# A table of 256 x 16,384 expert weights: written by GpSimd's accumulating indirect transfers instead of by one-hot products on TensorE

## What is computed

```python
qry = (af @ w_q).reshape(n, PEER_HEADS, 2, PEER_KEY_DIM)            # 8 heads
s = jnp.einsum('nhpd,hpkd->nhpk', qry, sub_keys)                    # two times 128 keys
s_top, i_top = lax.top_k(s, PEER_TOPK)                              # 16 of 128, twice
cand = s_top[:, :, 0, :, None] + s_top[:, :, 1, None, :]
sc, ci = lax.top_k(cand.reshape(n, PEER_HEADS, 256), PEER_TOPK)     # 16 of 256 pairs
experts = e_a * PEER_N_KEYS + e_b                                   # 8 x 16 = 128 per token
gw = jax.nn.softmax(sc, axis=-1)
act = jax.nn.gelu(jnp.einsum('td,tkd->tk', xb, u_tab[experts]))
out = jnp.einsum('tk,tkd->td', gw * act, v_tab[experts])
```

## Time and profile before

| | before |
|---|---|
| median of 3 runs | 1804.25 us (1803.99 to 1805.73) |
| span of the profiled execution | 1795.7 us |
| PE busy | 1744.2 us, 97% |
| DVE, ACT, POOL busy | 1251.2, 942.1, 492.9 us |
| TensorE's granted clock, mean | 0.994 |
| DMA bytes | 347.63 MB, mean 194 GB/s |

### The profile page before, as it was taken

How to read it: one execution, slowest core, us unless ns; L and a number is a source line. 1 busy time by engine, 2 the same in 40 slices (tenths; PEclk the granted TensorE clock), 3 DMA queues, 4 the chain that set the end, 5 groups by cost and what they waited for, 6 DMA issues and landing times.

```text
span 1795.7 us, 33010 instructions
## 1 busy us (share of the span) xinstructions
PE 1744.2 (97%) x11190; PEld 1547.2 (86%) x11190; DVE 1251.2 (70%) x2359; ACT 942.1 (52%) x1389; POOL 492.9 (27%) x225
## 2 busy tenths in 40 slices
PE   9999989999999999999999999999999999999997
PEld 6799878897878999999999988888888787669996
DVE  4567587876424499067777578888888896667777
ACT  5466577544555544567777643333333575334444
POOL 4246744401568588800000000000000100013332
PEclk9999999999999999999999999999999999999999
DMA  6654443577344478755565687677767783355553
GB/s 216 200 188 141 166 152 118 190 248 266 121 164 150 135 222 228 228 179 172 174 173 173 195 263 239 235 235 236 237 239 236 272 276 122 113 176 187 183 183 113
DMA packets 122839, 347.63 MB, mean 194 GB/s; under 512 B 13904, under 2 KB 46800, under 8 KB 122512
## 3 DMA queue, kind: packets, MB, share of 16 engines
q1 hardware_dynamic: 121248, 339.52, 58.1%
q0 software_dynamic: 1520, 7.21, 1.1%
HBM read 328.84 MB, written 17.83 MB: 193 GB/s over the span
## 4 chain that ended last, share of the span: by engine, by line
PE 84%; DVE 6%; ACT 4%; issue 2%; POOL 2%; DMA 1%; POOLq 0%; DVEq 0%; ACTq 0%
PE banks L934 83%; POOL weight_rest L851 2%; ACT arena L1676 2%; DMA weight_ring<-in_stream 1%; ACT weight_high L1676 1%; PE banks L945 1%; DVE weight_rest L2307 1%; ACT span_exponentials L1676 0%; DVE arena L3110 0%; DVE arena L2991 0%; DVE arena L2348 0%; ACT scratch L1676 0%; ACT L1676 0%; DVE arena L2347 0%; DVE arena L2345 0%
## 5 line engine op out<-in xcount | busy, mean ns | idle before, releaser
L1676 ACT ACTIVATE weight_high<-weight_ring 128x1024 fp32r<-128x1024 f32 x448 | 473.0, 1057 | 453.4 <-PE banks L934 350.4
L851 POOL TENSOR_TENSOR weight_rest<-weight_ring,weight_high 128x1024 fp32r<-128x1024 f32 x165 | 414.4, 2521 | 264.5 <-ACT weight_high L1676 155.0
L2307 DVE TENSOR_TENSOR weight_rest<-weight_ring,weight_high 128x1024 fp32r<-128x1024 f32 x283 | 346.1, 1224 | 156.3 <-ACT weight_high L1676 153.4
L934 PE MATMUL banks<-a_high,weight_high 128*128 128x256 f32 x1216 | 304.0, 288 | 0.2 <-ACT weight_high L1676 0.2
L934 PE MATMUL banks<-a_rest,weight_high 128*128 128x256 f32 x1216 | 297.8, 283 | 0.0
L934 PEld LDWEIGHTS banks<-a_high,weight_high 128*128 128x128 f32 x1216 | 232.6, 191 | 1.5 <-issue 1.1
L934 PEld LDWEIGHTS banks<-a_rest,weight_high 128*128 128x128 f32 x1216 | 232.9, 192 | 0.3 <-issue 0.2
L934 PE MATMUL banks<-weight_high,gated_high 128*128 128x512 f32 x512 | 201.4, 393 | 0.0
L934 PE MATMUL banks<-weight_high,gated_rest 128*128 128x512 f32 x512 | 200.2, 391 | 0.0
L934 PE MATMUL banks<-a_high,weight_rest 128*128 128x256 f32 x1216 | 170.9, 283 | 2.4 <-POOL weight_rest L851 2.4
L934 PE MATMUL banks<-x_high,weight_high 128*128 128x256 f32 x672 | 167.5, 287 | 4.7 <-DVE x_rest L3079 3.7
(11 more groups left out here) (360 smaller groups left out, 3101.5 us busy)
## 6 DMA issues: line engine op xcount, KB each, us to landing
weight_ring<-in_stream SPq DMA_DIRECT2D x512, 512.0 KB, 3.5
arena<-in_stream SPq DMA_DIRECT2D x66, 512.0 KB, 3.3
unit_spill<-small SPq DMA_DIRECT2D x128, 128.0 KB, 3.6
scratch<-unit_spill SPq DMA_DIRECT2D x128, 128.0 KB, 3.2
residual<-in_x SPq DMA_DIRECT2D x2, 512.0 KB, 4.1
arena<-in_mem POOLq DMA_DIRECT2D x2, 512.0 KB, 5.3
arena<-in_ctx POOLq DMA_DIRECT2D x2, 512.0 KB, 4.8
arena<-in_keys POOLq DMA_DIRECT2D x1, 1024.0 KB, 5.2
```

The costliest lines, as they stand in the source:

```text
L851: nc.gpsimd.tensor_tensor(w_lo[:, e % 2, :], raw(e)[0], w_hi[:, e % 2, :], ALU.subtract).then_inc(S["rest_ready"], 1)
L934: return nc.tensor.matmul(out, lhsT, rhs, start=start, stop=stop, skip_group_check=True)
L1676: return nc.scalar.activation(out, in_, f, **kw)
L2307: tt(w_lo[:, e % 2, :], raw(e)[0], w_hi[:, e % 2, :], ALU.subtract).then_inc(S[ready], 1)
```

## The change

G is built in DRAM. SP first fills `gate_matrix` (16.8 MB) with zeros, in 32 transfers of 512 KB from a block of 64 zeros per partition, one with every third tile of the early stream. DVE makes for each token and choice a number `expert * 256 + token`. POOL makes rests for 36 unit tiles only; then it issues 256 indirect transfers, one for each half of the tokens and each of the 128 choices. Each adds 128 weights, one from each partition, to 128 cells of `gate_matrix`. The 16 choices of a head name different experts; between the heads of one half it waits until the earlier transfers of that half have landed, so that sums are not lost. SP waits for all of them at the first value tile and then loads one row of G (128 KB) beside every value tile. `u2`, the transposes `eTr`, the one-hot matrices and the moves to `WT` are gone; DVE makes the rests of the last 92 unit tiles. Some semaphores are merged.

```diff
-U_EARLY, U_EXP, U_GATED = 52, 48, 64
+U_EARLY = 36
+N_ZERO = 32
@@ SP
+            def load_gates(a):
+                if a >= 4:
+                    sp.wait_ge(g_in[a % 4], 16 * (a // 4))
+                sp.dma_start(WT[:, a, :], gate_matrix[a]).then_inc(g_in[a % 4], 16)
+                if g == 32:
+                    sp.wait_ge(S["warm_zeros"], 2)
+                if g >= 32 and g % 3 == 0 and (g - 32) // 3 < N_ZERO:
+                    sp.dma_start(to_zero[(g - 32) // 3], zeros).then_inc(zeroed, 16)
                 if sec == "values":
                     if i < 6:
                         store_units(P - 6 + i)
+                    if i == 0:
+                        for t in range(TT):
+                            sp.wait_ge(scattered[t], 16 * PSLOT)
+                        for d in range(2):
+                            freed(sp, ("cH", d))
+                        for a in range(3):
+                            load_gates(a)
+                    if i + 3 < P:
+                        load_gates(i + 3)
@@ POOL, behind the rests of the first 36 unit tiles
+            pool.wait_ge(zeroed, 16 * N_ZERO)
+            cells = gate_matrix.rearrange("a b (t o) -> (a b t) o", o=1)
+            for h in range(PH):
+                for t in range(TT):
+                    if h == 0:
+                        pool.wait_ge(S["idx_ready"], t + 1)
+                    else:
+                        pool.wait_ge(scattered[t], 16 * PTOP * h)
+                    for k in range(h * PTOP, (h + 1) * PTOP):
+                        pool.indirect_dma_start(
+                            cells, bass.IndirectOffsetOnAxis(EXPERT_TOKEN[:, t, k:k + 1], 0), EAB[:, t, 2, k:k + 1], None,
+                            compute_op=ALU.add).then_inc(scattered[t], 16)
@@ PE
-            for t in range(TT):
-                pe.wait_ge(S["idx_ready"], t + 1)
-                transposes(("eTr", t), [EAB[:, t, x, :] for x in range(3)])
-            with pe.Fori(0, T // 16) as i:
-                for u in range(4):
-                    units(U_EARLY + u, ("u2", u), i)
...
-                    for v in range(4):
-                        ins = mm(b[:, hsl(v)], COLUMN[:, u % 2, v, :], ROWHOT[:, u % 2, v, :])
             with pe.Fori(0, U_LATE // 4) as i:
                 for j in range(4):
-                    units(U_EARLY + U_GATED + j, ("u3", j), i)
+                    units(U_EARLY + j, ("u3", j), i)
@@ DVE, with the early rests
+            step(V.tensor_reduce(token_numbers[:, 0:1], C("upto"), AX.X, ALU.add))
+            for t in range(TT):
+                ts(token_numbers[:, 1 + t:2 + t], token_numbers[:, 0:1], -1.0, float(P * (t + 1)), ALU.mult, ALU.add)
@@ DVE, end of best_pairs
+                step(stt(OH[:, 0:P], EAB[:, t, 0, :], float(P), EAB[:, t, 1, :], ALU.mult, ALU.add))
+                step(ts(EXPERT_TOKEN[:, t, :], OH[:, 0:P], float(T), token_numbers[:, 1 + t:2 + t], ALU.mult, ALU.add))
@@ DVE, behind the searches
+            split_rest(UD, "lo_ready")
             gates(0)
             gates(1)
-            with dve.Fori(0, T // 16) as i:
-                for u in range(4):
-                    split_rest(UD + u, "lo_ready", i, 4)
...
+            for j in range(1, 4):
+                split_rest(UD + j, "lo_ready")
+            with dve.Fori(0, U_LATE // 4 - 1) as i:
+                for j in range(4, 8):
+                    split_rest(UD + j, "lo_ready", i, 4)
@@ DVE, gate_row
                 dve.wait_ge(h_in[s], i_ * 16 + 16 * (a // 4 + 1))
+                dve.wait_ge(g_in[s], i_ * 16 + 16 * (a // 4 + 1))
```

More of the change, by code:

```diff
@@ L336, in plan_banks @@
     B.loop("u1", U_EARLY // 4, 4, banks=(4, 5, 4, 5))
-    for t in range(TT):
-        B.job("eTr", t, bank=6 + t)
     for d in range(2):
         B.job("cH", d, bank=4 + d)
-    B.loop("u2", U_GATED // 4, 4, banks=(4, 5, 4, 5))
-    B.loop("w", T // 16, 4, banks=(6, 7, 6, 7))
-    B.loop("u3", U_LATE // 4, 4, banks=(4, 5, 6, 7))
+    B.loop("u3", U_LATE // 4, 4, banks=(4, 5, 4, 5))
     B.job("ad1", "rows", 2, bank=4)
@@ L529, in build @@
         h_in = [sem(f"units_loaded{s}") for s in range(4)]
+        g_in = [sem(f"gates_loaded{s}") for s in range(4)]
+        zeroed = sem("gate_matrix_zeroed")
+        scattered = [sem(f"gates_scattered{t}") for t in range(TT)]
         in_x = [sem(f"x_loaded{t}") for t in range(TT)]
@@ L809, in load_units @@
                 sp.dma_start(UNITS_IN[:, a % 4, :], spill[a]).then_inc(h_in[a % 4], 16)
+            def load_gates(a):
+                if a >= 4:
+                    sp.wait_ge(g_in[a % 4], 16 * (a // 4))
+                sp.dma_start(WT[:, a, :], gate_matrix[a]).then_inc(g_in[a % 4], 16)
+            zeros = bass.AP(zero_block[:, :].tensor, zero_block[:, :].offset, [zero_block[:, :].ap[0], [0, 16], [1, 64]])
+            to_zero = gate_matrix.rearrange("a b t -> (a b t)").rearrange("(p n r c) -> n p r c", p=P, n=N_ZERO, c=64)
             for g in range(len(RING_TILES)):
@@ L889, in _ @@
                     split_rest(U0 + j, i, 4)
+            pool.wait_ge(zeroed, 16 * N_ZERO)
[10 more added lines that the diff above has]
+                            compute_op=ALU.add).then_inc(scattered[t], 16)
             for s in range(4):
                 pool.wait_ge(h_out[s], 16 * P // 4)
-            pool.dma_start(FIN1, A["fin1"].partition_broadcast(P)).then_inc(in_gain, 16)
+            pool.dma_start(FIN1, A["fin1"].partition_broadcast(P)).then_inc(in_second, 16)
             arrived(pool, ("x2T", 1, 1))
@@ L898, in _ @@
             pool.dma_start(GSPAN[:, :, :], A["span"]).then_inc(in_second, 16)
-            pool.wait_ge(in_second, 4 * 16)
+            pool.wait_ge(in_second, 5 * 16)
             pool.wait_ge(S["x2_lo_ready"], 4)
@@ L1807, in _ @@
             act.wait_ge(S["dt_abs"], 1)
-            func(NEGA, row("a_log"), ACT.Exp).then_inc(S["neg_a"], 1)
+            func(NEGA, row("a_log"), ACT.Exp).then_inc(S["dt_l"], 1)
             step(func(DTS, DTS, ACT.Exp, scale=-1.0))
@@ L2036, in _ @@
                 split_high(U0 + j + 2)
-            with act.Fori(1, U_EXP // 4) as i:
+            with act.Fori(1, U_EARLY // 4) as i:
                 for j in range(4):
@@ L2044, in _ @@
                 func(EAB[:, t, 2, :], EAB[:, t, 2, :], ACT.Exp).then_inc(S["gate_exp"], 1)
[L2045 to L2051 removed]
             for d in range(2):
                 evacuate(("cH", d), h0[:, d], src=quarters)
[L2055 to L2084 removed]
             with act.Fori(0, U_LATE // 4) as i:
                 for j in range(4):
[L2087 removed]
+                    act.wait_ge(h_out[j], i * 16 + 16 * U_EARLY // 4)
                     unit_out(("u3", j), j, i)
[L2089 removed]
+                    split_high(U0 + U_EARLY + j + 2, i, 4)
             with act.Fori(0, P // 4 - 1) as i:
@@ L2768, in _ @@
             gate_scores(1)
+            split_rest(UD, "lo_ready")
             gates(0)
             gates(1)
-            for t in range(TT):
-                freed(dve, ("eTr", t))
-            ts(slots[:, 3, :], slots[:, 1, :], -1.0, None, ALU.mult).then_inc(S["slots_negated"], 1)
-            with dve.Fori(0, T // 16) as i:
-                for u in range(4):
-                    split_rest(UD + u, "lo_ready", i, 4)
-                    b, n = B.at[("w", (u - 2) % 4)]
-                    dve.wait_ge(bank_full[b], i * 2 + (n if u >= 2 else n - 2))
-                    for v in range(4):
-                        slot = bass.ds(i * 16 + (4 * u + v), 1)
-                        ins = ts(ROWHOT[:, u % 2, v, :], C("iota"), slots[:, 0, slot], slots[:, 2, slot],
-                                 ALU.is_equal, ALU.mult)
-                    ins.then_inc(S["onehot_ready"], 1)
-                    if u:
-                        quad = bc(slots[:, 1, bass.ds(i * 16 + 4 * u, 4)], 2, P)
-                        tt(COLUMN[:, u % 2], bc(C("iota"), 1, 4), quad, ALU.is_equal).then_inc(S["dve_columns"], 1)
-            with dve.Fori(0, U_LATE // 4) as i:
-                for j in range(4):
-                    split_rest(UD + U_GATED + j, "lo_ready", i, 4)
-            for u in range(4):
-                freed(dve, ("w", u), T // 16 - 1)
+            for j in range(1, 4):
[3 more added lines that the diff above has]
+                    split_rest(UD + j, "lo_ready", i, 4)
             def gate_row(a, turn=None):
```

82 lines of the change are left out of this document (21 added, 61 removed).

## The result

The changed kernel takes **2023.55 us** (median of 4 runs, 2022.43 to 2026.78) against 1804.38 us before (4 runs, 1803.99 to 1805.73): 1.1219 times the time, 95% interval 1.1203 to 1.1235. The prediction said 1775.6 us, 1747 to 1895. It missed by 248 us, and the time lies outside its range. The profiled execution has a span of 2021.2 us.

A forecast was written before the change was run, and what follows sets the result against it. PE was taken to bound the kernel, with 84% of the chain that ended last. 1804.25 - 56.8 (PE's work) + 2.5 (small things) + 25.6 (waiting for POOL's transfers) = 1775.6 us; range 1747 to 1895.

The forecast's parts named there:

- The bound and the gain: Units stage: PE bounds it; 56.1 us from u2 and the transposes eTr, together 56.8 us less; late tiles at 2.88 us.
- The shape of the wait: PE before the first value product: 726.0 + 256 x + 9.5 - 991.6, so 256 x - 256, if above zero.
- tail: From POOL's last issue to the first value product: landing 5.0 us, load of G's row 0 3.2, `gate_row` 1.3; 9.5 us.
- x: Time per indirect transfer issued by POOL: estimated 1.10 us, giving 25.6 us of waiting; break-even 1.21, all hidden below 1.00.
- Rival 3: First load of G: POOL late by more, slower from x = 1.22; 1865 us at 1.45, 1903.5 at 1.60; chance 0.34.
- Rival 4: Units stage: DVE's rests shut out POOL's issues, leaving POOL 58% of the time; 138 us of waiting, 1888 us; chance 0.08.
- Small things: Token numbers, cell numbers, zeros and loads of G across the kernel: 2.5 us added in all.
- Token numbers: Three tiny DVE operations beside the reduction at 60.55, on the chain: 0.5 us added.
- Loads of G in the values stage: One row of G per value tile adds 0.4 us of DMA time each; room remains, 1 us in all.
- Zeros: 32 transfers of 512 KB in the tile queue, 1.6 us each by bytes, mostly hidden by prefetch; 1 us in all.
- rival 5: DMA engines: zeros priced by 256-byte pieces, 14 us a block, 446 us for 32; early stages stretch 150 us or more; chance 0.04.

## Why the prediction was wrong, point by point

- **The bound and the gain: right.** PE's stream in the units stage shrank by 57.4 us, 56.8 forecast; the late tiles run 2.88 us apart with all rests on DVE.
- **The shape of the wait: right, its terms partly.** Wait = start + transfers + tail - end of units. The start came at 738.2 for 726.0: 10.4 us of it is the early delay, 1.8 us stands on DVE, where the weights follow the rest at 735.35. The tail was 4.8 us for 9.5 (POOL's last issue ends at 1263.87, SP loads at 1265.34, PE starts at 1268.66): the 5.0 us of landing was a 512 KB transfer's, and counted from its issue, where these 128 elements land 2.96 us from theirs, 1.4 us behind its end. The end of units was 1001.5 for 991.6.
- **x: the step that failed.** "I take two direct issues, 1.10 us [...], since a list of descriptors that depends on data and reads two operands is about twice the work of a plain one." The list without addition costs 1.26, with it 1.85, on average beside DVE 2.055. From first to last start 524 us passed, where 282 were forecast, and PE waited 267.2 us for 25.6: 242 of the 248 us missed. The dearest case that I priced, three direct issues, 1.60 us, lies below even the bare price. It was worked out as reads and writes of the same kind, one per operand; the run with 64 rows shows that the price is hardly one of elements at all, so counting operands couldn't bound it. What the fixed part is spent on, no row shows.
- **Rival 3** (POOL late by more, 0.34) is what happened, beyond the price I gave it: with x = 1.85 alone the formula gives 256 x 1.85 - 256 = 218 us. **Rival 4** (shut out by DVE's rests, 0.08) happened on top of it, milder: the rests take a fifth of POOL's pace (2.30 for 1.85), not the 42% of their share in time. It cost 48 us (the run with short rests). It is milder because an issue waits only when it begins inside a rest, not in all the time of the rests. And the low chance of this rival rested on the row of 1056.44, which could show no such wait (above). I had treated the two as alternatives with chances that add; they are two factors of one product, and the range should have reached to the product. The Trainium skill (SBUF — State Buffer, "A bandwidth-pool intuition that's wrong (but worth ruling out)") has descriptor writing of GpSimd wait for DVE. The rows agree for the indexed form: an issue that begins inside a rest ends later by what is left of it, less 0.13 us, and 2.57 us is the longest. For the direct form beside these rests they don't (0.579 us at most).
- **The Trainium skill's emission figure** (DMA: Bandwidth & Descriptors, "Latency and other measured facts", about 1 us) stands between the direct form here (0.54) and the indexed accumulating one (1.85); neither is 1 us. It is a figure up to the first byte, and these are distances between issues, so it was no price for x.
- **Small things.** Token numbers: 0.5 us forecast; PE's wait at 60 us grew from 2.5 to 3.0 us. Loads of G in the values stage: 1 us forecast; 119 value tiles take 330.92 us between ACT's roundings (from 1291.04 on) for 329.99 before (from 1067.08), 0.9 us more. Zeros: 1 us forecast, most of 10.4 measured, of which some 3.5 for the first four blocks and 3.8 in 340 to 420 (the rest is mixed with the 2 us by which executions differ). I had priced a block by bytes (1.6 us of all engines) and had the price by pieces as rival 5; the truth lies between, and what I left out is that two stretches, 90 to 125 and 340 to 420, have tiles that PE waits for at once.
- **A term that no step had:** the restart. While PE idles the granted clock is 0.50 (1.2 GHz), in 1268 to 1275 it is 0.60 on average, from 1280 on 1.00 (2.4 GHz), and the values stage is 4.6 us longer: 0.9 of drift, 3.7 at its start. From its first product to the second tile's products with weight_rest 7.30 us pass (1268.66 to 1275.96) for 4.63 before (1048.30 to 1052.93): 2.7 us at the low clock, where products stand 0.43 us apart in place of 0.23. Another 0.9 us is lost by 1288, at full clock, where PE waits for a rest (0.5 us) while the transfers that stood behind SP's wait catch up (DMA share 1.01).

With the measured terms the sum closes: 1804.4 - 57.4 + 10.4 + 267.2 + 4.6 + 0.6 = 2029.8 us, less 6.3 for the gap between span and median, 2023.5.

**Would a version beat both?** The direct kernels show the ceiling, 1746 to 1755 us, but a direct transfer can't reach cells that the search finds. Even without any disturbance by DVE 256 x 1.85 = 474 us have to pass from 738 on, and the units stage ends at 1001. Sharing the work (one token half by transfers, the other by one-hot products) would give half the gain back, 28 us, and between two heads POOL would wait for a landing (2.96 us at the end of the kernel after) that the other half's transfers hide now, 7 x 3 = 21 us. With 6 us more beside DVE's rests that is 27 us later than in the run with half of the transfers, whose end of units, 28 us later now, still comes first: 1788 + 27 = 1815 us, less up to 5 us for half of the zeros, an estimate. That is argued; it wasn't run.

## What to carry to other kernels

Price a new instruction form before relying on hiding 256 of it: here direct, accumulating and indexed transfers of the same 128 elements cost 0.54, 0.87 and 1.85 us, and no row of the old form bounded the new. When work moves to an engine behind a barrier, write the wait as start + n x + tail - end, give x an upper end far beyond the nearest rows where none of them has the new form, and multiply disturbances into it instead of pricing them apart. Before a row is taken to show that two engines don't disturb each other, look how much of the one operation was left when the other began. Fill-in DMA traffic is free only where every stretch that it crosses has room: look at the DMA share window by window, and use long pieces.

## What the runs showed of the hardware that I had not expected

- An indexed GpSimd transfer with the addition has an almost fixed price: 1.41 us with 64 elements, 1.55 with 128, and 0.30 us of idle behind each.
- An addition costs more in the indexed form (0.59 us) than in the direct one (0.33 us).
- An indexed issue that begins inside one of DVE's 128x1024 operations, of two sources or of one, takes longer by what is left of it less 0.13 us; one that is under way, or begins within 0.04 us of the operation, isn't lengthened. A direct issue isn't lengthened beside the two-source rests. What comes out as 0.57 us per rest hangs on the phase: it is 0.33 with the issues of 64 elements.
- Indexed writes without the addition stop the other queue's loads almost wholly (12 GB/s over 295 us), near or far cells alike, and for some 20 us more after the last issue (25 with far cells).
- Filling with 256-byte pieces gave a DMA share of 0.95 at 279 GB/s where 2048-byte pieces gave 0.88 at 300 (340 to 420 us).
